# A two-block transformer kernel: the S5 recurrence over 128 chains of four tokens, run among projections and gated attention, with modulation rows loaded in half panels

## The reference

```python
mod = silu(c) @ ada_w + ada_b                    # 6*1024 columns; second block: the same with w_mod, for 2 vectors
hn = rmsnorm(h, mix_pre_g) * (1 + sc1) + sh1
q, k, v, og, a_lr, u = split(hn @ w_in)          # 256, 256, 512, 512, 16, 512 columns
o = gla_chunked(q, k, v, log_a(a_lr))            # gated linear attention, 4 heads, 8 chunks of 64 tokens
gla_out = rmsnorm(o, gla_norm_g) * silu(og)
# S5: 32 groups of 16 channels, 64 complex states each; x_t = A x_{t-1} + B u_t, A diagonal
y = C_re @ x_re - C_im @ x_im + d * u
s5_out = gelu(y) * sigmoid(gelu(y) @ glu_w + glu_b)
mix = concat(gla_out, s5_out) @ w_out
h = h + g1 * rmsnorm(mix, mix_post_g)
ff = moe_ffn(rmsnorm(h, ffn_pre_g) * (1 + sc2) + sh2)    # top 4 of 32 experts, 402 MB of weights
h = h + g2 * rmsnorm(ff, ffn_post_g)
# then the second block (window and grid attention, SSM, convolutional FFN)
```

## Time and profile before

| | us |
|---|---|
| median of 3 runs (3575.67 to 3578.99) | 3577.45 |
| the profiled execution | 3579.49 |
| its span | 3577.7 |
| PE busy | 3186.9 |
| DVE busy | 1169.6 |
| ACT busy | 520.2 |
| POOL busy | 268.4 |

### The profile page before, as it was taken

One profiled execution on the slowest core, in us unless ns is written; L12 is line 12 of the kernel. 1 busy time (PEld: TensorE's weight loads), 2 busy tenths in 40 slices (PEclk: granted clock), 3 DMA queues, 4 the chain that ended last, 5 costly groups with the idle time before them and its releaser, 6 DMA issues.

```text
span 3577.7 us, 33491 instructions
## 1 busy us (share of the span) xinstructions
PE 3186.9 (89%) x13492; PEld 1528.5 (43%) x13493; DVE 1169.6 (33%) x2030; ACT 520.2 (15%) x990; POOL 268.4 (8%) x352
## 2 busy tenths in 40 slices
PE   5967678999999999999994988787878999999998
PEld 2442234444443333333332644456556444444444
DVE  1348952332233332323233247324143001212201
ACT  1211012100000000010102124213133000100000
POOL 0026521000000000000000003000000000000000
PEclk8969778799999999999996899987889999999999
DMA  9216331699999999999982110110100222121210
GB/s 273 71 33 235 139 108 36 222 326 338 335 328 353 357 353 356 351 361 348 356 326 84 48 36 1 42 36 1 48 1 1 71 83 94 65 76 59 77 65 24
DMA packets 287682, 582.43 MB, mean 163 GB/s; under 512 B 7953, under 2 KB 12492, under 8 KB 287500
## 3 DMA queue, kind: packets, MB, share of 16 engines
q1 hardware_dynamic: 281328, 562.19, 44.0%
q0 software_dynamic: 5072, 15.80, 1.9%
q10 hardware_dynamic: 1132, 2.30, 0.2%
HBM read 576.08 MB, written 4.19 MB: 162 GB/s over the span
## 4 chain that ended last, share of the span: by engine, by line
PE 79%; DVE 13%; ACT 3%; issue 2%; DMA 1%; POOL 1%; SPq 0%; DVEq 0%; ACTq 0%; PEldq 0%; POOLq 0%
PE psum_all L211 76%; DVE scratch L1235 4%; PE psum_all L219 3%; DVE hidden L2078 2%; DMA panel<-in_ada_w 1%; DVE scratch L1259 1%; DVE scratch L3140 1%; DVE scratch L1252 1%; ACT scratch L3202 1%; DVE scratch L2726 1%; SPq L188 0%; ACT hidden L433 0%; DVE resid L1331 0%; ACT scratch L410 0%; ACT scratch L412 0%
## 5 line engine op out<-in xcount | busy, mean ns | idle before, releaser
L211 PE MATMUL psum_all<-panel,scratch 128*64 128x512 f32 (+3 forms) x5568 | 977.0, 507 | 1.4 <-ACTq L1853 0.8
L211 PE MATMUL psum_all<-hidden,panel 128*128 128x512 f32 (+1 forms) x1808 | 796.9, 602 | 21.5 <-ACT hidden L433 10.9
L211 PEld LDWEIGHTS psum_all<-hidden,panel 128*128 128x128 f32 (+1 forms) x1808 | 347.3, 193 | 462.3 <-issue 444.2
L211 PEld LDWEIGHTS psum_all<-panel,scratch 128*64 128x64 f32 (+2 forms) x5568 | 333.7, 131 | 472.2 <-issue 425.6
L211 PE MATMUL psum_all<-scratch 128*128 128x64 f32 (+8 forms) x1512 | 366.7, 440 | 111.6 <-DVEq L1273 63.6
L211 PEld LDWEIGHTS psum_all<-scratch 128*128 128x128 f32 (+2 forms) x1512 | 232.0, 234 | 212.9 <-DVEq L1273 77.0
L2078 DVE TENSOR_TENSOR hidden<-hidden,psum_all 128x512 f32<-128x512 f32 x264 | 169.7, 684 | 290.5 <-PE psum_all L211 290.5
L211 PE MATMUL psum_all<-scratch,panel 128*128 128x512 f32 (+1 forms) x672 | 250.5, 531 | 2.0 <-DVE resid L3327 1.0
L219 PE MATMUL psum_all<-const,scratch 128*128 128x128 f32 (+4 forms) x954 | 151.7, 298 | 84.1 <-ACTq L3214 22.8
L219 PEld LDWEIGHTS psum_all<-const,scratch 128*128 128x128 f32 (+4 forms) x954 | 110.5, 156 | 185.1 <-issue 84.0
L211 PEld LDWEIGHTS psum_all<-scratch,panel 128*128 128x128 f32 x672 | 127.5, 190 | 127.5 <-issue 119.6
(11 more groups left out here) (314 smaller groups left out, 2219.1 us busy)
## 6 DMA issues: line engine op xcount, KB each, us to landing
panel<-in_exp_w_gu SPq DMA_DIRECT2D x132, 2048.0 KB, 11.9
panel<-in_exp_w_down SPq DMA_DIRECT2D x66, 2048.0 KB, 14.2
panel<-in_w_in SPq DMA_DIRECT2D x17, 2048.0 KB, 8.5
panel<-in_ada_w SPq DMA_DIRECT2D x12, 2048.0 KB, 9.1
panel<-in_w_mod SPq DMA_DIRECT2D x12, 2048.0 KB, 8.0
panel<-in_ffn_w_gate SPq DMA_DIRECT2D x5, 2048.0 KB, 7.8
panel<-in_ffn_w_up SPq DMA_DIRECT2D x5, 2048.0 KB, 7.8
panel<-in_w_out SPq DMA_DIRECT2D x4, 2048.0 KB, 7.9
```

The lines of the kernel that those rows point to most:

```text
L211: ins = self.pe.matmul(out, lhsT, rhs, start=start, stop=stop)
```

## The change

S5 works on four pairs of groups at once, and on chains: token 4n+j is step j of chain n, so a row of 512 columns holds 4 pairs of 128 chains. B's powers for the four steps are put into one weight (`e_in`, K = 4 steps of 32 channels), so that one matmul of 128 columns for a pair gives each chain's input, and DVE scans 128 chains with the fourth power of A. What passes between the four tokens of one chain goes through a Toeplitz block (`toep`) of C A^k B on PE; C's powers are `ca`. The four-step loop replaces the 16 pairs. u is moved from features by tokens into steps by chains by 32 small SBUF to SBUF DMAs, y back by 16. In `pe_mix` the parts of S5 stand between the projections; the modulation rows stand between og, GLU, and attention's heads. The angles and factors of S5 (`dve_s5_angles`, `dve_s5_factors`) come before the first norm, the projection of u before the others, and the first norm's squares and sum beside the first rows. The 20 later rows have a ring of two half panels of 1 MB in slot 2 (`row_ring`): 12 come in `pe_mix` (`pe_tail_row`), 2 after the norm of mix (`NORM_ROWS`), 4 and 2 in routing (`ROUTE_ROWS`, `SLOT_ROWS`). `s5_log_dt` is loaded as 32 elements and spread by PE; x is loaded by SP ahead of the first panels.

```diff
-            for p in range(S5_PAIRS):
-                for i in range(2):
-                    pe.wait_ge(to_dve.free, to_dve.room())
-                    bank = to_dve.fill()
-                    mm(bank[:, :], s5_b[i][:, p, :], u_t[:, p // 4, :]).then_inc(to_dve.full, 1)
-
-                for i, (vectors, _, _, n) in enumerate(rows_of_step(p)):
-                    pe_mod_row(pe, mm, mod_banks, vectors, n)
-                    if i == 0 and p:
-                        outputs(p - 1)
-                    pe_mod_turn(pe, mm, mod_banks, mod_row2, n)
...
+        def pe_row(pe, mm, row):
+            vectors = (c_first, c_second)[row[0]]
+            halves = [row_ring.use(STRIPS, 512) for _ in range(2)]
...
+        def pe_s5_states(pe, mm, q4):
...
+                for m in range(4):
+                    ins = mm(bank[:, m * CHAINS:(m + 1) * CHAINS], e_in[:, 4 * q4 + m, c, :], u4[:, 4 * q4 + m, :])
...
+        def pe_s5_outputs(pe, mm, q4):
...
+                mm(bank[:, m * CHAINS:(m + 1) * CHAINS], toep[:, p, :], u4[:, p, :], True, False)
+                for c in range(2):
+                    ins = mm(bank[:, m * CHAINS + 1:(m + 1) * CHAINS], ca_flat[c][:, p, 32:32 + P],
+                             x_out[q4 % 2][c][:, m * CHAINS:(m + 1) * CHAINS - 1], False, c == 1)
...
+            pe_s5_setup(pe, mm)
+            pe_s5_states(pe, mm, 0)
+            pe_s5_kernels(pe, mm)
+            pe_s5_states(pe, mm, 1)
+            s, w = pe_panel(pe, dense_ring, DT, 512)
+            pe_tile(pe, mm, to_act, w, hidden, T, 0, DT)
+            pe_tile(pe, mm, to_act, w, hidden, T, 1, DT)
+            pe_s5_outputs(pe, mm, 0)
+            pe_s5_states(pe, mm, 2)
...
+            pe_tail_row(pe, mm, 4)
+            pe_tile(pe, mm, to_act, glu_w, y, T, 2, 4)
+            pe_tile(pe, mm, to_act, glu_w, y, T, 3, 4)
+            pe_tail_row(pe, mm, 5)
+            pe_head(pe, mm, 0)
+            pe_tail_row(pe, mm, 6)
+            pe_head(pe, mm, 1)
+            pe_head_sums(pe, mm, 0)
...
+            for j in range(CHAIN - 2, -1, -1):
+                e_re, e_im = (e_pad[:, :, i, j + 1, :] for i in range(2))
+                tt(t1, e_re, are, ALU.mult).then_inc(dve_done, 1)
...
+                for m in range(4):
+                    own = slice(m * CHAINS, (m + 1) * CHAINS)
+                    mag4 = s5c[:, S5_MAG4, 4 * q4 + m:4 * q4 + m + 1].broadcast_to([P, CHAINS])
+                    dve.tensor_tensor_scan(z[:, own], mag4, w[:, own], 0.0, ALU.mult, ALU.add).then_inc(dve_done, 1)
...
+            dve_decay_rates(dve)
+            dve_s5_setup(dve, step)
+            dve_s5_step(dve, step, 0)
+            dve_decay_sums(dve, step)
+            dve_s5_diagonal(dve, step)
+            dve_s5_step(dve, step, 1)
+            dve_keys(dve, step)
+            dve_s5_step(dve, step, 2)
+            dve_keys_to_end(dve)
+            dve_s5_step(dve, step, 3)
+            dve_states(dve, step)
...
+            for m in range(4):
+                for j in range(CHAIN):
+                    sp.dma_start(u4[32 * j:32 * j + 32, 8 * half + m:8 * half + 8:4, :],
+                                 u_perm[32 * m:32 * m + 32, 2 * half:2 * half + 2, j, :]).then_inc(u_moved[half].sem, 16)
```

More of the change, by code:

```diff
@@ L482, in pe_mod_row, with pe_panel, pe_tile @@
-        def pe_mod_row(pe, mm, banks, vectors, n):
-            s, w = panels.use(DT, 512)
-            pe.wait_ge(panels.loaded[s], panels.arrived(s))
+        def pe_panel(pe, ring_, k_tiles, width):
+            s, w = ring_.use(k_tiles, width)
+            pe.wait_ge(ring_.loaded[s], ring_.arrived(s))
+            return s, w
+        def pe_tile(pe, mm, banks, w, x, n, m, k_tiles, c=P, by_tile=None):
+            pe.wait_ge(banks.free, banks.room())
+            bank = banks.fill()
+            for k in range(k_tiles):
+                if by_tile is not None:
+                    pe.wait_ge(by_tile.sem, by_tile.next(pe))
+                ins = mm(bank[0:c, 0:n], w[:, k, m * P:m * P + c], x[:, k, 0:n], k == 0, k == k_tiles - 1)
+                if k == k_tiles - 1:
+                    ins.then_inc(banks.full, 1)
@@ new lines, in pe_token_tile, with pe_linear @@
+        def pe_token_tile(pe, mm, banks, w, x, t, k_tiles):
+            pe.wait_ge(banks.free, banks.room())
+            bank = banks.fill()
+            for k in range(k_tiles):
+                ins = mm(bank[:, :], x[:, k, t * P:(t + 1) * P], w[:, k, :], k == 0, k == k_tiles - 1)
+                if k == k_tiles - 1:
+                    ins.then_inc(banks.full, 1)
+        def pe_linear(pe, mm, ring_, banks, x, n, k_tiles, width):
+            s, w = pe_panel(pe, ring_, k_tiles, width)
+            for m in range(width // P):
+                pe_tile(pe, mm, banks, w, x, n, m, k_tiles)
+            mm.done(ring_.used[s])
@@ new lines, in pool_s5, with act_s5_steps @@
+        def pool_s5(pool, step):
+            pool_s5_zeros(pool)
+            pool_s5_bases(pool, step)
+            for q4 in range(4):
+                pool_s5_table(pool, step, q4)
+        def act_s5_steps(act):
+            act.wait_ge(to_act.full, to_act.next_full())
+            bank = to_act.take()
+            act.activation(s5c[:, S5_DT, :], bank[:, 0:S5_PAIRS], ACT.Exp).then_inc(to_act.free, 1)
+            act.wait_ge(to_act.free, to_act.own_reads())
+            act.sem_inc(s5_cols.sem, 1)
@@ new lines, in act_u @@
+        def act_u(act):
+            for half in range(2):
+                for q4 in range(2 * half, 2 * half + 2):
+                    act.wait_ge(to_act.full, to_act.next_full())
+                    bank = to_act.take()
+                    act.activation(u_perm[:, q4, :, :], bank[:, :].rearrange("p (n j) -> p j n", j=CHAIN),
+                                   ACT.Copy).then_inc(to_act.free, 1)
+                act.wait_ge(to_act.free, to_act.own_reads())
+                act.sem_inc(moves_ready.sem, 1)
@@ new lines, in act_s5_setup @@
+            act.wait_ge(act_done, step.next(CHAIN - 1))
+            act.sem_inc(s5_blocks.sem, 1)
+            act.wait_ge(s5_zeroed.sem, s5_zeroed.next(act, 4))
+            for b in range(4):
+                act.wait_ge(to_act.full, to_act.next_full())
+                bank = to_act.take()
+                b4 = bank[:, :].rearrange("p (g x) -> p g x", x=P)
+                for j in range(CHAIN):
+                    own = slice(32 * j, 32 * j + 32)
+                    ins = act.activation(toep[own, 4 * b:4 * b + 4, 32 * j:P], b4[own, :, 0:P - 32 * j], ACT.Copy)
+                    if j == CHAIN - 1:
+                        ins.then_inc(to_act.free, 1)
+                    else:
+                        ins.then_inc(act_done, 1)
@@ L1135, in pe_s5, with pe_s5_steps, pe_s5_setup @@
+        def pe_s5_steps(pe, mm):
+            pe.wait_ge(s5_setup.sem, s5_setup.next(pe))
+            pe.wait_ge(to_act.free, to_act.room())
+            bank = to_act.fill()
+            for two in range(2):
+                ins = mm(bank[64 * two:64 * two + 64, 0:S5_PAIRS], of_parity[:, two:two + 1].broadcast_to([2 * S5_PAIRS, 64]),
+                         dt_of_pair)
+            ins.then_inc(to_act.full, 1)
+        def pe_s5_setup(pe, mm):
             pe.wait_ge(s5_loaded.sem, s5_loaded.next(pe, 16 * 8))
@@ L2051, in dve_moe @@
                 if u == 0:
+                    dve_second_mods(dve, step)
                     dve_extra_lists(dve, step)
```

1411 lines of the change are left out of this document (813 added, 598 removed).

## The result

The changed kernel takes 3476.18 us (median of 4, 3463.65 to 3479.95), the kernel before 3576.56 in its 4 runs: ratio 0.9712, interval 0.9686 to 0.9739. It is faster by 100, where the forecast was 149 faster (3428) and the range ended at 3463. The profiled execution took 3473.6, its span 3471.6.

The account below looks back on a forecast made before the run. DVE bounded S5's 16 pairs, and the expert stage would keep its length. 3577.7 - 189.7 (earlier out-projection) + 40 (eight rows added before the experts) = 3428 us; range for 8 in 10: 3398 to 3463.

Parts of the forecast that it names:

- the front's mechanism: Before the projections: slow s5_log_dt loads delay the ada_w rows; loading 32 elements instead starts projections at 48, not 71.63.
- End of the blocks' wait: In S5, before the blocks: DVE makes the powers of B, then of C, while PE waits some 9, until 103.5.
- The rival that gives time back in the experts: Experts: delay rows replace idle-time panel loads, the stage may grow by 18; 3446 to 3480, chance 0.04.
- In all +40: Out-projection to first expert: eight added rows cost +6.5 after the norm of mix, +22 in routing, +11.7 before the slots.
- 10.1 after the start: Routing: row 15 ends 10.1 us after the start, its second half landing behind its first.
- The period of the rows that have a turn between them: Rows bound by their half panels: reload after four matmuls, 5.4 + 1.0 + 0.2 = 6.6 us a row.
- cold term: Ahead of the out-projection: half of some 12 rows and heads at the low clock level, about 8 us.
- the rival's 3450: From 241 on: clock stays low through heads and rows, 22 us more, 3450; shares chance 0.18 with slower half panels.
- The term for the three expert panels ahead of row 9: SP's queue: row 9's halves wait behind three expert panels, 3 x 5.2 plus its own 2 MB, until 303.
- 51 operations without a wait: S5 factors on DVE: 51 of 111 operations have no wait, saving 0.1 each, so 18 us instead of 23.0.
- The rival "more is saved": Added rows fill waits and keep the clock up in routing, and the front starts at 43: 3400, chance 0.18.
- The rival of slow half panels: Twelve waiting rows: half panels cost up to 8.0 instead of 5.4, +31: 3459; shares chance 0.18 with the low clock.

Follow-up runs that it names:

- the edit of the kernel before: Kernel before the change, with the two loads of s5_log_dt waiting until a panel of w_in has landed: 3559.70 us, ratio 0.9958.
- the release in time: Changed kernel, with each modulation row's second half panel given back by a drain right behind the row's last matmul: 3466.57 us, ratio 0.9699.
- the deep version: Changed kernel, with rows 9 to 19 loaded as whole panels four deep, expert panels behind row 19, and early buffer release: 3408.47 us, ratio 0.9531.

## Why the prediction was wrong

**Right.** The bound and its removal; the front's mechanism (last panel used at 35.68, forecast near 32; projections 45.18, forecast 48; the late `s5_log_dt` loads were held to be the cause, which the edit of the kernel before shows). End of the blocks' wait 105.42 (103.5), steps of 10.8 us (11 to 12), expert stage of the same length. The rival that gives time back in the experts is out.

**The step that failed most: the eight added rows, "In all +40".** The stage grew by 65.2. By the prediction's own terms it would be 183.7 long, with PE busy for the 125.4 of before and 24 more (8 rows at 3.0), and so idle for 34.3. It was busy for 162.9 and idle for 46.0: 11.7 of the 25.2 that were missing are waits, 13.5 are slower matmuls.

The waits: the prediction let row 15 end "10.1 after the start (its second half lands behind its first)". From 470.11 it ended at 486.93, 16.8 after. I took a half to be released by its own last matmul; the signal of the second one is owed to the next matmul, which three times, at rows 13, 15 and 19, is one that waits. With the release in time row 15 ends 12.0 after the start and PE is idle for 37.5 in the stage, so 8.5 of the 11.7 are this. The period of the rows that have a turn between them was near: 7.1 (487.06 to 494.17 for row 16), not 6.6, by a half row that took 1.94 and not 1.0.

The slower matmuls: the prediction priced the eight rows at the high level of the clock and put its cold term ahead of the out-projection only. In the trace a half row takes 1.93 and two turns 3.57, and the eight rows keep PE busy for some 40 us, not 24.

Both hang on the loads. Without them 58 us go, 35.5 of waits and 23.0 of matmul time, far more than the 25 that were missing, since the forecast too had landings on the path: it never asked whether the rows could be loaded earlier, under the out-projection.

**The cold term, "about 8 us".** It was under-sized and left out of the norm and routing. Ahead of the out-projection the window 276 to 347 stands at 0.62: two of the four heads take 5.23 instead of 2.84 (4.8 more), four turns 1.86 instead of 1.05 (3.2), six half rows 1.93 instead of 1.06 and two rows 3.15 and 2.64 instead of 1.92 (7.1), three pairs of head sums 2.07 instead of 1.12 (2.9). That is 18, part of which lies under the next half's landing. So the rival's 3450, a clock that stays low through heads and rows, was right in kind ahead of the out-projection; what it lacked is the routing. The Trainium skill, page "TensorE: Matmul & The Clock Gate", section "HAM oscillation — how this bites in real kernels", has short groups of matmuls with a DMA wait between them fall back to the low clock each time. The traces agree for the rows (0.58 from 470 to 532, 0.93 from 460 to 484 where the same rows have no loads). The 0.50 of the router's matmuls, which wait for nothing, is another case.

**The other misses ahead of the out-projection** are sums of small ones. Of the 21.2 the kernel is 7.7 late at 203, 13.3 at the GLU product (254.61 for 241.3), and the rest follows behind it, with the cold term's 8 already in the forecast: 6 us by 136 (blocks at 8.74 instead of 6.9, waits of 1.78 and less, states that ran slower), 1 more until 163, and at row 3 a wait of 6.11 and 0.71 where 4 was given, with that row and its turn at the low level. The term for the three expert panels ahead of row 9 was near: about 20 was forecast from row 8 to row 9, and it is 22. The front came out 3 early, since the factors took 16.6 and not 18 and the first shifted tile came 2 sooner; the last `ada_w` panel, 4 later than forecast, wasn't what the norm waited for. The forecast counted 51 operations without a wait; the code has 54.

The rival "more is saved" said that added rows fill waits and keep the clock up. With the loads in time that is what they do: 14 us for eight rows in the deep version, whose 3408 is near that rival's 3400. In the kernel as it is the loads come too late for it. The rival of slow half panels is out: a half lands in 5.1 to 5.2.

**Left open.** How the deep version's 65 us split between the depth of the ring and the order of the loads. Why the router's matmuls stay at the low level. What makes the changed kernel's runs differ by 0.5%: of the 7.6 us between the spans of its two traces 5.0 lie ahead of the out-projection, and no run tried why.

## What to carry over

A filler that needs a transfer fills nothing unless the transfer is early. Count for it one landing per buffer that isn't deep enough, and read in the code which instruction carries the signal that frees the buffer: one that rides on the next instruction is as late as that instruction's own wait. Look then at when the idle DMA engines could have loaded it; here they were all but idle (a share of 0.02) for the 57 us of the out-projection, and four slots instead of one, with the release and the order of loads mended, were worth 65 us.

## What was not expected of the hardware

- 54 semaphore waits between DVE operations of 16 columns cost some 7 us, 0.13 each.
- Over rows 14 to 19 PE, busy 38.70 of 54.97 us, had a granted clock of 0.57; with work of no use in its waits, busy 48.33 of 53.65, it had 0.87, and the stretch was 1.3 us shorter.
- In the router's matmuls PE is busy for 13.64 of 13.64 us with a granted clock of 0.50.
